# Inverted 16x16 blocks leave for DRAM and come back without the zeros between them, and are spread on chip

## The chip, the core and the metric

The kernel runs on one core of a Trainium2 chip. The metric is the device time of one execution in microseconds (us). The kernel before took 2705.86 us as the median of 3 runs (2704.35 to 2707.13).

## The reference, cut to what matters

One inference step of a trunk of two layers, for a prompt of 1024 tokens and a group of 8 samples of 4 tokens each. Layer 0 mixes with gated DeltaNet heads (and a spatial gate beside them), layer 1 with mLSTM heads; each is followed by a squared-ReLU MLP. The change lies in the DeltaNet heads alone: 4 heads, keys and values of 128.

```python
def gated_delta_rule(q, k, v, g, beta, S0):
    ...                                     # blocks of C tokens, gc = running sum of g
    kb = k * beta[..., None]
    A = jnp.where(strict, jnp.einsum('nbhid,nbhjd->nbhij', kb, k) * decay, 0.0)
    rhs = jnp.concatenate([v * beta[..., None], kb * jnp.exp(gc)[..., None]], -1)
    sol = lax.linalg.triangular_solve(jnp.eye(C) + A, rhs, left_side=True, lower=True, unit_diagonal=True)
    u_val, w_k = sol[..., :DV], sol[..., DV:]
    ...
    def step(S, xs):
        v_new = u_c - jnp.einsum('bhik,bhkv->bhiv', wk_c, S)
        o = jnp.einsum('bhik,bhkv->bhiv', qd_c, S) + jnp.einsum('bhij,bhjv->bhiv', qk_c, v_new)
        S = S * gl_c[..., None, None] + jnp.einsum('bhik,bhiv->bhkv', kd_c, v_new)
        return S, o
```

What matters is the solve with the lower triangle I + A, once for each block of tokens and each head. The kernel takes blocks of 128 tokens and computes the inverse itself.

## The kernel before, in words

**Two kinds of work.** The large matrix products (`dense` in PSUM) run with f32 inputs split into a high and a low half: ScalarE makes `whi` from a weight block that SyncE has loaded into `wst` (L1112), VectorE makes `wlo = wst - whi` (L1623), and TensorE multiplies high by high, low by high and high by low (L587). A weight block of 128x1024 is a *unit*. A unit on the first group of 512 tokens or on the second of 544 (512 + 32 sample tokens) is cut into four *pieces* (`("d", u, p)`), each of two of the eight inner steps: 6 matmuls of 512 columns, or 12 of 272. The heads' work (`mixer` in PSUM, `arena` in SBUF) is written as a second list of items.

**The order.** `Plan.mix` lays the second list evenly among the pieces of the first; an item `("rest",)` is a place with nothing in it. Every engine walks the same list in order and does its own part of each item, with semaphores between them, so the list sets the order on every queue. An engine that waits holds up all that stands behind on its own queue.

**DeltaNet by tiles.** `Plan.gdn` writes the items of each prompt tile of 128 tokens (tiles 0 to 7; tiles 0 to 3 lie beside the input projection, tiles 4 to 7 beside the first MLP). For tile t:

- `sum`, `dec`, `kk`, `kT`, `vT`: norms, decays, and A (TensorE L587, VectorE L1887).
- `kk` on GpSimd (`base_blocks`): A is written to `arow` in DRAM (L2446), and its 32 diagonal 16x16 blocks (4 heads, 8 each) are read back with one block on each of 32 partitions (L2448) into `C`.
- `b1`, `b2`, `b3` on VectorE: the 32 blocks are inverted by substitution and merging (L1845, L1847), and a transposed copy `CT` is made (L1922), which counts up the semaphore `g_inv`.
- `b3` on GpSimd: after `g_inv` it writes `C` and `CT` to the diagonals of eight 128x128 matrices `xrow` in DRAM (L2453, twice), whose other places were set to zero at the start (L2320). When both have landed it reads all eight matrices back (L2456) into `XX`: 4 plain ones (`Xi`) and 4 transposed (`XiT`).
- `la`, `lb` for the levels 4, 5 and 6: the inverse grows from blocks of 16 to 32, 64 and 128. TensorE's `la` of level 4 waits for `g_bin`, the landing of the read. VectorE masks (L1936) and adds (L1943).
- `vn`, `zw`, `o`, `oT`: the inverse meets the right-hand sides, the state `St` is carried on.

Between `b3` and the first `la` stand 3 rests. The memory of `C`, `CT` and of the scratch belongs to `SQ` and `RB` of the tile, which the next tile's `act` item (ScalarE, `w("bout", ...)`) writes again.

Of the kernel before, what the change touches and what calls it, by code (L numbers as in the profile page):

```python
# [7 lines left out]
ALU = mybir.AluOpType  # L8
# [67 lines left out]
class Plan:  # L76
# [64 lines left out]
    @staticmethod  # L141
    def gdn(tiles):
        out = []
        for i, t in enumerate(tiles):
            if i == 0:
                out += [("gx", t), ("g", t, "act", 0)] + [("g", t, "gv", 0)] * (t >= 4) + [("g", t, "sum", 0)]
            out += [("g", t, s, 0) for s in ("dec", "kk", "kT")] + [("rest",)]
            out.append(("g", t, "vT", 0))
            more = i + 1 < len(tiles)
            if more:  # L150
                out.append(("gx", t + 1))
            out += [("rest",)] * 1 + [("g", t, s, 0) for s in ("b1", "b2", "b3")] + [("rest",)] * 3
            for q in range(LB, LEVELS):
                out += [("g", t, "la", q), ("g", t, "lb", q)]
                if q == 4 and more:
                    out.append(("g", t + 1, "act", 0))
                if q == 5 and more and t + 1 >= 4:
                    out.append(("g", t + 1, "gv", 0))
            if i == 0:
                out += [("gx2", t), ("rest",), ("rest",)]  # L160
            out += [("g", t, s, 0) for s in ("vn", "zw", "o")]
            out.append(("g", t + 1, "sum", 0) if more else ("rest",))
            out.append(("g", t, "oT", 0))
            if more:
                out.append(("gx2", t + 1))
        return out
# [148 lines left out]
def build(nc, x_prompt, x_sample, state_gdn, state_gdn_conv, state_mlstm_c, state_mlstm_n, state_mlstm_m,  # L315
# [4 lines left out]
    with ctx:  # L320
# [7 lines left out]
        def sb(name, shape, dt=F32):  # L328
            return ctx.enter_context(nc.sbuf_tensor(name, shape, dt))
# [42 lines left out]
        cum = sb("cum", [P, TILES + 1, 12])  # L372
        epsc = sb("epsc", [P, 1])
        fold = sb("fold", [4 * H, 2 * H])
        ssx = sb("ssx", [P, TILES + 1])


# [39 lines left out]

        def inv_at(t, q, p):

            return t * (1 + 2 * NL) + (2 * (q - LB) + p + 2 if t < TILES else 2 * q + p + 1)  # L420

        def t2_at(t, q, p):

# [6 lines left out]
        def gdn_map(t):  # L430
            n = P if t < TILES else NS
            keys = ["X", "QH", "SQ", "RB", "DT", "QD", "XX", "KB", "KD", "RU", "VB"]
            shapes = [(NCH, n), (8, n), (8, n), (8, n), (H, n), (H, n), (2, 4, n), (H, n)] + [(H, P)] * 3
            if n == NS:
                keys += ["RW", "NW", "NWM", "QDM", "KM", "SS"]
                shapes += [(H, P), (H, n), (H, NB, NS), (H, NB, NS), (2, 4, P), (2, NB, P)]
            m = dict(zip(keys, carve(arena, *shapes)))
            m["Dm"], m["E"] = m["SQ"][:, 0:4], m["SQ"][:, 4:8]
            m["T2"], m["A"] = m["RB"][:, 0:4], m["RB"][:, 4:8]
            m["ON"], m["VN"] = m["VB"] if n == P else m["RW"], m["RU"]  # L440
            m["Xi"] = lambda h: m["XX"][0:n, 0, h, :]
            m["XiT"] = lambda h: m["XX"][0:n, 1, h, :]
            if n == P:
                sq, t2 = (m[k].rearrange("p h n -> p (h n)") for k in ("SQ", "RB"))
                m["C"], m["CT"], m["U"] = carve(sq[0:NBLK], (CB,), (WB * WB,), (WB * WB // 4,))
                m["tmp"] = t2[0:NBLK, 0:512]
            return m

# [53 lines left out]
        mrow = nc.dram_tensor("mrow", (2, 2, H, GN[1]), F32)  # L502
        grow = nc.dram_tensor("grow", (H, T), F32)
        arow = nc.dram_tensor("arow", (H, P * (P + 1)), F32)
        xrow = nc.dram_tensor("xrow", (2 * H, P * (P + 1)), F32)

        def by_token(rows):

# [76 lines left out]
        def _(pe):  # L585
# [171 lines left out]
            def gdn(t, step, q):  # L757
# [58 lines left out]
                elif step == "la":  # L816

                    r, c0 = half(q, n)
                    for p in range(2):
                        if q == LB:  # L820
                            w("bin", 32 * (t + 1))
                            if p:
                                w("ru")
                        else:
                            w("inv", inv_at(t, q - 1, p))
                        for h in (2 * p, 2 * p + 1):
                            last = mm(M4(3 * p)[0:r, h % 2, 0:r], m["A"][0:n, h, 0:r], m["XiT"](h)[:, c0:n])
                        s(last, "t2")
                        if q == LEVELS - 1:
                            for h in (2 * p, 2 * p + 1):  # L830
                                last = pe.transpose(M4(1 + p)[0:r, h % 2, 0:n], m["XiT"](h)[:, 0:r], ident[0:n, 0:n])
                            s(last, "xt")
# [270 lines left out]
        def _(act):  # L1103
# [251 lines left out]
            def gdn(t, step, q):  # L1355
# [5 lines left out]
                if step == "act":  # L1361
                    w("xin", 32 * (t + 1))
                    if t:
                        w("qd", t)
                        w("bout", 48 * t + 16)
                    if g:
                        after(own(A_(X[:, 0:12, :], X[:, 0:12, :], ACT.Silu)))
                    s(A_(m["SQ"], X[:, 0:8, :], ACT.Square), "sq")
# [233 lines left out]
        def _(dve):  # L1602
# [256 lines left out]
            def gdn(t, step, q):  # L1859
# [58 lines left out]
                elif step == "b3":  # L1918
                    if LB == 4:
                        merge_right(m, 0, 8)  # L1920
                    c = m["C"][:, 0:WB * WB].rearrange("p (i j) -> p i j", j=WB)
                    s(dve.tensor_copy(m["CT"].rearrange("p (j i) -> p i j", i=WB), c), "inv")  # L1922
                elif step == "l0":
                    for p in range(2):
                        w("t2", t2_at(t, 0, p))
# [333 lines left out]
        def _(pool):  # L2259
# [48 lines left out]
            def constants():  # L2308
# [7 lines left out]
                pool.memset(rowmask[:, :], 1.0)  # L2316
                pool.memset(colmask[:, :, :], 0.0)
                pool.memset(lmask0T[:, :], 0.0)
                step(pool.memset(lmask[:, :, :], 0.0))
                dma(by_token(xrow[:, :]), lmask[:, 0:1, :].broadcast_to([P, 2 * H, P]))\  # L2320
                    .then_inc(S("g_bout"), 16)
                for m, n in ((triU, P), (triUS, NS)):
                    step(affine(m[:, :], [[1, n]], ALU.is_ge, 0.0, 0, -1))
                for m, n in ((maskpos, P), (maskposS, NS)):
# [10 lines left out]
                    step(pool.memset(colmask[:, b, b * LS:(b + 1) * LS], 1.0))  # L2335
                v = lmask0T[:, :].rearrange("p (b e) -> p b e", e=2)
                step(affine(v[:, :, 0], [[-2, P // 2]], ALU.not_equal, 1.0, -1, 1))
                pool.wait_ge(S("g_bout"), 16)
                for q in range(LEVELS):
                    w = 1 << q  # L2340
                    v = lmask[:, q, :].rearrange("p (b e w) -> p b e w", e=2, w=w)
# [100 lines left out]
            def base_blocks(t, name):  # L2442
                m = gdn_map(t)
                if name == "kk":
                    pool.wait_ge(S("g_A"), t + 1)
                    dma(by_token(arow[:, :]), m["A"]).then_inc(S("g_bout"), 16)  # L2446
                    pool.wait_ge(S("g_bout"), 48 * t + 32)
                    dma(m["C"][:, 0:WB * WB].rearrange("p (i j) -> p i j", i=WB), diagonal(arow[:, :]))\  # L2448
                        .then_inc(S("g_bin"), 16)
                else:  # L2450
                    pool.wait_ge(S("g_inv"), t * (1 + 2 * NL) + 1)
                    for a, k in enumerate(("C", "CT")):
                        dma(diagonal(xrow[a * H:(a + 1) * H, :]), m[k][:, 0:WB * WB].rearrange("p (i j) -> p i j", i=WB))\  # L2453
                            .then_inc(S("g_bout"), 16)
                    pool.wait_ge(S("g_bout"), 48 * t + 64)
                    dma(m["XX"].rearrange("p a h n -> p (a h) n"), by_token(xrow[:, :])).then_inc(S("g_bin"), 16)  # L2456

            def gdn(t, name, q):
                if t < TILES and name in ("kk", "b3"):
                    base_blocks(t, name)  # L2460
                elif name == "vT":
                    n = tok(t)[2]
                    VB = gdn_map(t)["VB"]
# [194 lines left out]
```

## Time and profile before

| | |
|---|---|
| median of 3 runs | 2705.86 us (2704.35 to 2707.13) |
| the profiled execution | 2705.05 us, span 2703.3 us |
| mean granted TensorE clock | 0.983 |
| TensorE busy | 2597.3 us (96%) |
| VectorE busy | 1380.7 us (51%) |
| ScalarE busy | 1125.0 us (42%) |
| GpSimd busy | 256.4 us (9%) |
| HBM | 120 GB/s over the span |

Engines are named PE (TensorE; PEld is its weight load), DVE (VectorE), ACT (ScalarE), POOL (GpSimd) and SP (SyncE). L with a number is the line of the kernel. All matrix products have the line L587 of a helper, so they are told apart by what they write and read: `dense` or `mixer`. The granted clock is 1.00 at 2.4 GHz and 0.50 at 1.2 GHz; a stretch in between has parts of both. All scratch of the heads is one tile, `arena`, so its rows need the line or the shape to be told apart.

### The profile page before, as it was taken

To read this page: it belongs to the slowest core of one execution; us is meant where nothing else is said; L and a number is where in the kernel's file an instruction comes from. 1 tells how busy PE (TensorE), PEld (TensorE's weight loads), DVE (VectorE), ACT (ScalarE), POOL (GpSimd) and SP (SyncE) were. 2 spreads that over 40 slices of the span, in tenths; PEclk is the share of its full clock that TensorE was granted. 3 is DMA by queue.
4 is the path that set the end of the run, shared out by engine and by line. 5 is a ranking of instruction groups with operands and counts; after the bars stand their busy time and mean duration, and the time that the engine had idled before them with its cause. 6 is when DMAs were issued, how large, how long until landed. Compare 5 with 4: busy or idle time off the path is not lost.

```text
span 2703.3 us, 39205 instructions
## 1 busy us (share of the span) xinstructions
PE 2597.3 (96%) x16262; PEld 2311.4 (86%) x16262; DVE 1380.7 (51%) x2193; ACT 1125.0 (42%) x1913; POOL 256.4 (9%) x408
## 2 busy tenths in 40 slices
PE   7988979999999999999999999999999999999998
PEld 5767878777778788899999998998877797999998
DVE  4745664645655366534444456535554447344344
ACT  5553446544545245433333345434332344332334
POOL 5021111101101001110000001110000000000000
PEclk9998989999999999999999999999999999999999
DMA  6554324524433335543333335554434334233232
GB/s 197 158 150 120 109 85 120 171 83 114 115 95 90 94 117 176 177 147 102 98 102 102 100 87 169 170 155 125 121 121 125 114 109 134 87 109 110 88 92 80
DMA packets 370017, 325.65 MB, mean 120 GB/s; under 512 B 12074, under 2 KB 339812, under 8 KB 369841
## 3 DMA queue, kind: packets, MB, share of 16 engines
q1 hardware_dynamic: 336224, 207.91, 26.7%
q0 software_dynamic: 33616, 115.25, 14.1%
q8 instruction: 129, 2.11, 0.3%
q14 instruction: 48, 0.39, 0.0%
HBM read 265.00 MB, written 58.10 MB: 120 GB/s over the span
## 4 chain that ended last, share of the span: by engine, by line
PE 77%; DVE 6%; ACT 3%; DMA 2%; issue 1%; POOL 0%; DVEq 0%; ACTq 0%; POOLq 0%
PE dense L587 68%; PE mixer L587 7%; DVE wlo L1623 1%; DMA arena<-xrow 1%; ACT arena L1112 1%; DVE arena L1845 1%; ACT whi L1112 1%; DMA xrow<-arena 1%; DVE arena L1847 0%; DVE hf L1761 0%; ACT relu L1112 0%; DVE accA L1698 0%; DVE hlo L1757 0%; PE mixer L1033 0%; PE mixer L961 0%
## 5 line engine op out<-in xcount | busy, mean ns | idle before, releaser
L587 PE MATMUL dense<-hhi,whi 128*128 128x272 f32 (+1 forms) x3072 | 852.7, 332 | 20.1 <-DVE hlo L1757 10.1
L587 PE MATMUL dense<-hlo,whi 128*128 128x272 f32 (+1 forms) x3072 | 827.0, 323 | 0.0
L587 PE MATMUL dense<-hhi,wlo 128*128 128x272 f32 (+1 forms) x3072 | 826.8, 323 | 0.0
L1623 DVE TENSOR_TENSOR wlo<-wst,whi 128x1024 fp32r<-128x1024 f32 x384 | 472.0, 1229 | 239.5 <-ACT whi L1112 238.5
L587 PEld LDWEIGHTS dense<-hhi,whi 128*128 128x128 f32 x3072 | 517.5, 190 | 80.0 <-issue 15.3
L1112 ACT ACTIVATE whi<-wst 128x1024 fp32r<-128x1024 f32 x384 | 403.7, 1051 | 417.5 <-PE dense L587 413.9
L587 PEld LDWEIGHTS dense<-hhi,wlo 128*128 128x128 f32 x3072 | 516.0, 190 | 42.6
L587 PEld LDWEIGHTS dense<-hlo,whi 128*128 128x128 f32 x3072 | 518.5, 190 | 37.4 <-issue 0.7
L587 PE MATMUL dense<-h1hi,whi 128*128 128x272 f32 (+1 forms) x1536 | 425.1, 331 | 12.3 <-DVE wlo L1623 7.5
L587 PE MATMUL dense<-h1hi,wlo 128*128 128x272 f32 (+1 forms) x1536 | 415.2, 324 | 0.0
L587 PE MATMUL dense<-h1lo,whi 128*128 128x272 f32 (+1 forms) x1536 | 414.9, 324 | 0.0
L587 PEld LDWEIGHTS dense<-h1hi,whi 128*128 128x128 f32 x1536 | 256.6, 188 | 44.1 <-DVE wlo L1623 11.5
L587 PE MATMUL mixer<-arena 128*128 128x128 f32 (+11 forms) x1552 | 237.4, 299 | 54.2 <-DMA arena<-xrow 53.2
L1639 DVE TENSOR_TENSOR h1lo<-relu,h1hi 128x544 fp32r<-128x544 f32 (+1 forms) x128 | 90.6, 708 | 377.2 <-ACT relu L1112 377.1
L587 PEld LDWEIGHTS mixer<-arena 128*128 128x128 f32 (+5 forms) x1552 | 199.5, 178 | 94.6 <-DMA arena<-xrow 55.9
L587 PEld LDWEIGHTS dense<-h1lo,whi 128*128 128x128 f32 x1536 | 258.5, 189 | 21.3 <-issue 0.5
L587 PEld LDWEIGHTS dense<-h1hi,wlo 128*128 128x128 f32 x1536 | 256.6, 188 | 22.5
L1112 ACT ACTIVATE relu<-dense 128x512 f32<-128x512 f32 (+2 forms) x132 | 80.6, 611 | 408.3 <-PE dense L587 408.2
L1698 DVE TENSOR_TENSOR accA<-dense,accA 128x512 f32<-128x512 f32 (+1 forms) x168 | 116.5, 699 | 102.0 <-PE dense L587 101.6
L1112 ACT ACTIVATE ffh<-dense 128x512 f32<-128x512 f32 (+6 forms) x124 | 62.3, 526 | 193.5 <-PE dense L587 180.1
L1714 DVE TENSOR_TENSOR ssum<-ssum,sq 128x512 f32<-128x512 f32 (+1 forms) x98 | 69.3, 707 | 125.5 <-ACT sq L1112 125.4
L1112 ACT ACTIVATE arena<-mixer 128x128 f32<-128x128 f32 (+9 forms) x175 | 63.4, 377 | 99.6 <-PE mixer L587 58.1
(346 smaller groups left out, 1807.2 us busy)
## 6 DMA issues: line engine op xcount, KB each, us to landing
wst<-in_w_ff_dram SPq DMA_DIRECT2D x256, 512.0 KB, 4.0
wst<-in_w_in_even_dram SPq DMA_DIRECT2D x48, 512.0 KB, 4.1
wst<-in_w_in_odd_dram SPq DMA_DIRECT2D x48, 512.0 KB, 4.0
proj<-ffh POOLq DMA_DIRECT2D x48, 272.0 KB, 2.5
proj<-ffh POOLq DMA_DIRECT2D x48, 256.0 KB, 2.6
arena<-proj POOLq DMA_DIRECT2D x16, 512.0 KB, 4.9
wst<-in_w_out_even_dram SPq DMA_DIRECT2D x16, 512.0 KB, 3.7
arena<-proj POOLq DMA_DIRECT2D x8, 1024.0 KB, 7.9
```

The lines of the kernel that those rows point to most:

```text
L587: return pe.matmul(out, lhsT, rhs, start=start, stop=stop)
L1112: return act.activation(out, in_, func, **how)
L1623: TT(wlo[:, u % 2, :], wst[:, u % 2, :], whi[:, u % 2, :].bitcast(F32), ALU.subtract)\
L1639: TT(h1lo[:, k, 0:n], r, h1hi[:, k, 0:n].bitcast(F32), ALU.subtract)\
L1698: TT(v, out_of(key, g), v, ALU.add).then_inc(S("dve_evac"), 1)
L1714: ins = TT(ssum[:, 0:n], ssum[:, 0:n], sq2[:, c % 2, 0:n], ALU.add)
L1845: link(TT(tmp, left.unsqueeze(2).broadcast_to([NBLK, b, b, b]), right.rearrange("p j c -> p c j").unsqueeze(1).broadcast_to([NBLK, b, b, b ...
```

## The change

What goes to DRAM is one transfer for `C` and `CT` together, 32 partitions with two runs of 256 numbers, into an `xrow` that holds nothing but the blocks. What comes back is `D16`, 128 partitions with 8 runs of 16 numbers: for each of the 4 heads, plain and transposed, row i of block b on partition 16b + i. A new item `b4` multiplies it into `XX`: each run of 16 is repeated at the 8 block places of its row, times a mask `blkmask` (128x8) that is 1 where the row belongs to the block. VectorE does this for the transposed half, GpSimd for the plain half, and both count up `g_inv`; TensorE's first `la` waits for that count instead of the landing, and so does the next tile's `act` on ScalarE. The zeroing transfer at the start goes; a memset and two selects for the mask come. In the list of items, 5 rests and `b4` stand where 3 rests stood.

```diff
@@ Plan.gdn
-            out += [("rest",)] * 1 + [("g", t, s, 0) for s in ("b1", "b2", "b3")] + [("rest",)] * 3
+            out += [("rest",)] * 1 + [("g", t, s, 0) for s in ("b1", "b2", "b3")] + [("rest",)] * 5
+            out.append(("g", t, "b4", 0))
@@ places in SBUF and DRAM
+                m["both"] = sq[0:NBLK, 0:2 * CB].rearrange("p (a x) -> p a x", a=2)[:, :, 0:WB * WB]
+                m["D16"] = carve(sq, (2, H, WB), at=640)[0]
-        xrow = nc.dram_tensor("xrow", (2 * H, P * (P + 1)), F32)
+        xrow = nc.dram_tensor("xrow", (2, NBLK, WB * WB), F32)
@@ TensorE, la of level LB = 4
-                            w("bin", 32 * (t + 1))
+                            w("inv", t * (3 + 2 * NL) + 3)
@@ ScalarE, act of the next tile
-                        w("bout", 48 * t + 16)
+                        w("inv", inv_at(t - 1, LB, 0) - 1)
@@ VectorE
+                elif step == "b4":
+                    w("bin", 32 * t + 32)
+                    shape = [P, H, P // WB, WB]
+                    s(TT(m["XX"][:, 1].rearrange("p h (b j) -> p h b j", j=WB),
+                         m["D16"][:, 1].unsqueeze(2).broadcast_to(shape),
+                         blkmask[:, :].unsqueeze(1).unsqueeze(3).broadcast_to(shape), ALU.mult), "inv")
@@ GpSimd, base_blocks after b3
-                    for a, k in enumerate(("C", "CT")):
-                        dma(diagonal(xrow[a * H:(a + 1) * H, :]), m[k][:, 0:WB * WB].rearrange("p (i j) -> p i j", i=WB))\
-                            .then_inc(S("g_bout"), 16)
-                    pool.wait_ge(S("g_bout"), 48 * t + 64)
-                    dma(m["XX"].rearrange("p a h n -> p (a h) n"), by_token(xrow[:, :])).then_inc(S("g_bin"), 16)
+                    dma(xrow[:, :, :].rearrange("a p x -> p a x"), m["both"]).then_inc(S("g_bout"), 16)
+                    pool.wait_ge(S("g_bout"), 32 * t + 32)
+                    dma(m["D16"].rearrange("p a h j -> p (a h) j"),
+                        xrow[:, :, :].rearrange("a (h b) (i j) -> (b i) (a h) j", h=H, j=WB)).then_inc(S("g_bin"), 16)
@@ GpSimd, b4 (and the constants: blkmask made, the zeroing transfer taken out)
+                elif name == "b4":
...
+                    pool.wait_ge(S("g_bin"), 32 * t + 32)
+                    pool.tensor_tensor(m["XX"][:, 0].rearrange("p h (b j) -> p h b j", j=WB),
+                                       m["D16"][:, 0].unsqueeze(2).broadcast_to(shape),
...
+                        .then_inc(S("g_inv"), 1)
```

**What it does to the order.** In pieces of dense work in the list: between `b1` and the first `la` stood 6, 5, 5, 5, 10, 10, 10, 10 pieces for tiles 0 to 7, now 9, 7, 6, 7, 14, 14, 14, 14. From `vT` to the first `la` TensorE's queue had 54, 84, 72, 90, 90, 90, 78 dense matmuls for tiles 0, 1, 3, 4, 5, 6, 7 (tile 2 has the gate's products among them), now 66, 108, 96, 114, 108, 108, 102. The number of pieces is the same over the whole, so other gaps have fewer.

VectorE's queue in tile 5, from the transposed copy (L1922, now L1926) to the transpose after level 4. Before (`h1lo` is the low half of the MLP's hidden activations, one for each unit of its first product):

```order
L1922 COPY arena<-arena 32x16x16
L1639 TENSOR_TENSOR h1lo<-relu,h1hi 128x512
L1623 TENSOR_TENSOR wlo<-wst,whi 128x1024
L1639 TENSOR_TENSOR h1lo<-relu,h1hi 128x512
L1623 TENSOR_TENSOR wlo<-wst,whi 128x1024
L1936 TENSOR_TENSOR arena<-mixer,lmask 128x256 x2
L1943 TENSOR_TENSOR arena<-arena,mixer 128x256 x2
L1947 STREAM_TRANSPOSE arena<-arena 128x256 x2
```

And now:

```order
L1926 COPY arena<-arena 32x16x16
L1643 TENSOR_TENSOR h1lo<-relu,h1hi 128x512
L1627 TENSOR_TENSOR wlo<-wst,whi 128x1024
L1643 TENSOR_TENSOR h1lo<-relu,h1hi 128x512
L1627 TENSOR_TENSOR wlo<-wst,whi 128x1024
L1643 TENSOR_TENSOR h1lo<-relu,h1hi 128x512
L1930 TENSOR_TENSOR arena<-arena,blkmask 128x512
L1627 TENSOR_TENSOR wlo<-wst,whi 128x1024
L1946 TENSOR_TENSOR arena<-mixer,lmask 128x256 x2
```

One more unit's work stands between the copy and the first mask, and the spread of the transposed half (L1930) stands within it.

VectorE's queue in tile 1, from right behind the transposed copy on, where the dense work is the input projection with its convolution (`ffh<-ffh,par`). Before:

```order
L1653 COPY ffh<-ffh 128x3
L1656 COPY ffh<-ffh 128x8x3
L1623 TENSOR_TENSOR wlo<-wst,whi 128x1024
L1662 SCALAR_TENSOR_TENSOR ffh<-ffh,par 128x512
L1665 SCALAR_TENSOR_TENSOR ffh<-ffh,par 128x32
L1662 SCALAR_TENSOR_TENSOR ffh<-ffh,par 128x512
L1665 SCALAR_TENSOR_TENSOR ffh<-ffh,par 128x32
L1936 TENSOR_TENSOR arena<-mixer,lmask 128x256 x2
```

And now:

```order
L1666 SCALAR_TENSOR_TENSOR ffh<-ffh,par 128x512
L1669 SCALAR_TENSOR_TENSOR ffh<-ffh,par 128x32
L1677 COPY ffh<-ffh 128x3
L1678 COPY ffh<-ffh 128x24
L1657 COPY ffh<-ffh 128x3
L1660 COPY ffh<-ffh 128x8x3
L1627 TENSOR_TENSOR wlo<-wst,whi 128x1024
L1666 SCALAR_TENSOR_TENSOR ffh<-ffh,par 128x512
L1669 SCALAR_TENSOR_TENSOR ffh<-ffh,par 128x32
L1666 SCALAR_TENSOR_TENSOR ffh<-ffh,par 128x512
L1669 SCALAR_TENSOR_TENSOR ffh<-ffh,par 128x32
L1930 TENSOR_TENSOR arena<-arena,blkmask 128x512
```

One more step of the convolution stands ahead of the spread, and one step and the end of a unit behind it, ahead of the first mask.

GpSimd's queue in tile 5, from the loads of the next tile on. Before:

```order
L2402 DMA arena<-grow 128x4x128
L2453 DMA xrow<-arena 32x16x16 x2
L2456 DMA arena<-xrow 128x8x128
L2408 DMA arena<-proj 128x8x128
L2446 DMA arow<-arena 128x4x128
```

And now:

```order
L2412 DMA arena<-grow 128x4x128
L2462 DMA xrow<-arena 32x2x256
L2464 DMA arena<-xrow 128x8x16
L2474 TENSOR_TENSOR arena<-arena,blkmask 128x512
L2418 DMA arena<-proj 128x8x128
L2456 DMA arow<-arena 128x4x128
```

The two writes have become one, and the spread of the plain half stands right behind the read, with the late loads of the next tile behind it.

## Rows read from the trace of the kernel before

**Rows 1.** Waits of PE, longest first: total us, times, longest.

```profile
PE mixer L587 <- DMA arena<-xrow: 53.2, 8, 12.0
PE dense L587 <- DVE wlo L1623: 16.7, 15, 3.5
```

**Rows 2.** PE in order of time: start us, us, [idle before], tiles 0 to 7.

```profile
185.90 1.44 PE L587 MATMUL mixer<-arena 128*128 128x128 f32 x5 [9.97 <-DMA arena<-xrow]
...
253.40 1.86 PE L587 MATMUL mixer<-arena 128*128 128x128 f32 x7 [12.01 <-DMA arena<-xrow]
...
316.83 1.43 PE L587 MATMUL mixer<-arena 128*128 128x128 f32 x5 [3.51 <-DMA arena<-xrow]
...
378.58 1.65 PE L587 MATMUL mixer<-arena 128*128 128x128 f32 x6 [10.35 <-DMA arena<-xrow]
...
550.95 1.43 PE L587 MATMUL mixer<-arena 128*128 128x128 f32 x5 [5.39 <-DMA arena<-xrow]
...
644.02 1.37 PE L587 MATMUL mixer<-arena 128*128 128x128 f32 x5 [3.56 <-DMA arena<-xrow]
...
728.37 0.82 PE L587 MATMUL mixer<-arena 128*128 128x128 f32 x5 [1.66 <-DMA arena<-xrow]
...
811.75 1.65 PE L587 MATMUL mixer<-arena 128*128 128x128 f32 x6 [6.71 <-DMA arena<-xrow]
```

**Rows 3.** Stretches behind these waits: from:to, us, PE busy, granted clock, DMA share, GB/s.

```profile
185.90:192.00 6.10, 6.10 (x26) 0.65 0.00 0
253.40:260.00 6.60, 6.60 (x36) 0.62 0.11 43
316.83:322.00 5.17, 5.17 (x31) 0.71 0.04 8
378.58:386.00 7.42, 7.42 (x38) 0.59 0.26 72
550.95:557.00 6.05, 6.05 (x23) 0.63 0.10 27
644.02:649.00 4.98, 4.98 (x19) 0.66 0.25 87
811.75:817.00 5.25, 5.25 (x21) 0.71 0.01 3
```

**Rows 4.** PE in order of time, dense matmuls at full clock.

```profile
192.77 0.39 PE L587 MATMUL dense<-hlo,whi 128*128 128x512 f32 x1
193.00 0.40 PE L587 MATMUL dense<-hhi,wlo 128*128 128x512 f32 x1
```

**Rows 5.** POOL in order of time, tile 1.

```profile
245.38 1.32 POOL L2453 DMA_DIRECT2D xrow<-arena  x2 [1.68 <-DVE arena L1922]
248.80 0.89 POOL L2456 DMA_DIRECT2D arena<-xrow  x1 [2.11 <-DMA xrow<-arena]
```

**Rows 6.** DMA issues: queue, count, KB each, median us from issue to landing.

```profile
arena<-xrow POOLq DMA_DIRECT2D x8, 512.0 KB, 5.1
...
xrow<-arena POOLq DMA_DIRECT2D x16, 32.0 KB, 2.1
...
arena<-arow POOLq DMA_DIRECT2D x8, 32.0 KB, 2.2
```

**Rows 7.** Groups by shape from 140 to 830 us: count, busy us, mean ns, idle before.

```profile
L1662 DVE SCALAR_TENSOR_TENSOR ffh<-ffh,par 128x512 f32<-128x512 f32 x36 | 27.9, 775 | 0.4
...
L1897 DVE TENSOR_TENSOR arena<-arena 128x512 f32<-128x512 f32 x8 | 5.5, 682 | 0.0
...
L2467 POOL TENSOR_TENSOR arena<-arena 128x512 f32<-128x512 f32 x8 | 10.4, 1302 | 0.1
```

**Rows 8.** POOL and DVE in order of time, tile 1, an overlap.

```profile
234.22 1.30 POOL L2467 TENSOR_TENSOR arena<-arena 128x512 f32<-128x512 f32 x1
234.23 1.84 DVE L1662 SCALAR_TENSOR_TENSOR ffh<-ffh,par 128x512 f32<-128x512 f32 x1
```

**Rows 9.** Stretch before tile 3's wait, all engines: PE, PEld, DVE, ACT, POOL busy (x), clock, DMA.

```profile
340.00:372.00 32.00, 25.93 (x199) 24.35 (x197) 27.05 (x65) 18.41 (x50) 5.58 (x7) 0.99 0.34 95
```

## What the change will do, written before it ran

> **What bounds the kernel now.** I read the table of busy times first: TensorE works 2597.3 us of a span of 2703.3, so all its idle time together is 106 us, and no change off its path can pay more than that. The next view is TensorE's waits. Half of the idle time has one cause: the first `la` of each of the eight prompt tiles waits for the landing of `xrow`, 53.2 us in 8 waits; the next cause, the low halves of the weights, has 16.7 us [rows 1]. In order of time the eight waits are 9.97, 12.01, 3.51, 10.35 us (tiles 0 to 3) and 5.39, 3.56, 1.66, 6.71 us (tiles 4 to 7) [rows 2]. The reader is to see that the first four sum to 35.8 and the last four to 17.3.
>
> The stretches behind the waits show a second cost. TensorE is busy without a gap there, but at a granted clock between its two levels: 0.65, 0.62, 0.71, 0.59, 0.63, 0.66 and 0.71 [rows 3], where it is 1.00 soon after. After idle time TensorE runs on at 1.2 GHz for some us. Length times (1 - clock) is what that costs: 2.1, 2.5, 1.5, 3.0, 2.2, 1.7, 1.5, together 14.5 us. Tile 6, with the shortest wait, has none.
>
> So at most 53.2 + 14.5 = 68 us hang on these landings.
>
> **The sum, part by part.** I count against the profiled execution, 2705.05 us (span 2703.3 and 1.7 around it), which is 0.8 under the median.
>
> *1. More dense work ahead of `la`.* Consecutive matmuls of 512 columns start 0.23 us apart at full clock [rows 4], so a piece of 6 takes 1.38 us, and one of 12 by 272 columns about 1.46 (an estimate by columns).
>
> Tiles 4 to 7: from `b1` to `la` there are 14 pieces where there were 10, which is 5.5 us. VectorE reaches `b1` by the order of its queue there (A's blocks have long landed), so all that follows, the inverse and both transfers, runs against these pieces. 5.5 covers 5.39, 3.56 and 1.66; of 6.71 some 1 us may stay, less what the inverse gains from having one piece's work less between its own steps. I take 17.0 of 17.3. With the waits goes the low clock behind them: 2.2 + 1.7 + 1.5 = 5.4.
>
> Tiles 0 to 3: there the inverse hangs on `kk`, since `arow` goes out and comes back right before it and VectorE starts as soon as it can. From `vT` to `la` the dense matmuls rise by 12 (tile 0: 2 pieces of 1.38 = 2.8), by 24 of 272 columns (tile 1: 2.9) and by 24 (tile 3). In tile 3 one piece went away between `kk` and `kT`, so from `kk` it is one piece, 1.5; tile 2 also one, 1.5. Sum 8.7 of 35.8. The waits of tiles 0, 1 and 3 stay over 6 us each, and I leave the low clock behind them as it is.
>
> *2. The round trip.* In tile 1 GpSimd starts the writes at 245.38, the read at 248.80, and TensorE goes on at 253.40 [rows 5, 2]: 3.4 + 4.6 = 8.0 us. One issue instead of two saves half of the 1.32 that the pair takes, 0.66. The write has 64 KB in runs of 1 KB; a write of 32 KB in runs of 64 bytes lands in 2.1 [rows 6], and I expect no more. The read had 1024 runs of 512 bytes and landed in 5.1; now it has 1024 of 64 bytes. No row shows that shape. The nearest below is the read of `arow`, 512 runs of 64 bytes, 2.2; above, 5.1 if the count of runs sets the time. I take 3.3, nearer to the row with the same run. That saves 1.8 (0 to 2.9).
>
> DMA: Bandwidth & Descriptors (Specifications) in the Trainium skill speaks against this part: below 512 bytes a transfer is less than line rate, with read-modify-write. The run of 64 bytes is what it warns of; the rows show only that 512 such runs land in 2.2, less than half of what 1024 runs of 512 bytes take, and by the rule the upper end, 5.1, would be the likelier one: 1.8 more in each of four tiles, a sum of 21.1 and 2684.8, inside the forecast's own range.
>
> *3. The spread.* A VectorE product of two SBUF operands of 128x512 takes 0.68, GpSimd's takes 1.30 [rows 7]. In tiles 0 to 3 both engines are through with their earlier work when the read lands, and start together. What happens then can be seen in tile 1: GpSimd's product ran from 234.22 to 235.52, and a VectorE operation of 128x512 begun at 234.23 took 1.84 instead of its mean 0.775 [rows 8, 7]: it got hardly anything done until GpSimd had finished. So the pair costs 1.30 + 0.68 = 2.0 on the path, not 1.3. The repeated operands have no row; I bound it from 1.3 (no overlap) to 2.6 (each half as long again).
>
> This is what SBUF — State Buffer (Who interferes with whom) in the Trainium skill says: a VectorE instruction with two SBUF inputs contends with a GpSimd instruction that reads SBUF, and one blocks. By that rule, the trace agrees (1.84 against 0.775), and dividing the spread between the two engines saves nothing while they start together; without it the pair would take 1.30 and the sum would be 2.7 larger, 2675.
>
> The round trip with the spread: -0.66 - 1.8 + 2.0 + 0.1 for one more semaphore = -0.3 us per tile (bounds -2.2 and +2.1). It counts in tiles 0 to 3: 1.2 (from 8.8 down to -8.4). In tiles 4 to 7 GpSimd spreads at once and VectorE about a piece before `la`.
>
> *4. What it takes.* (a) `la` now depends on VectorE's place in its queue. In tiles 5 and 6 `b4` is one piece ahead of `la` (1.38 us), and VectorE first has an addition or a low half of 0.7 behind the piece before, then 0.68: about even. I take 0.5 per tile in tiles 4 to 7, 2 us in all (0 to 4). (b) The pieces come out of other gaps: between levels 4 and 5 tiles 4 and 7 have one piece between `la` and `lb` where they had two, between levels 5 and 6 some have none. The levels already run at one piece in tiles 0 to 3, with next to no wait there, so I take 0.25 per tile, 2 us (up to rival 2). (c) VectorE's 8 products are 5.5 us of an engine that is 51% busy, hidden but for (a). (d) The start: a transfer issue less, a memset and two small selects more on GpSimd, even.
>
> Sum: 17.0 + 5.4 + 8.7 + 1.2 - 2 - 2 = 28.3 us. From 2705.05 that is 2676.8, and 2677.6 on the footing of the median. Forecast 2678; its own range is 2670 to 2686 by the bounds of the trip and of 4.
>
> **Rivals.**
>
> *Rival 1, the round trip becomes much shorter.* The read lands in 2.2 and the spreads hardly disturb each other: -2.2 in each of tiles 0 to 3, 8.8 instead of 1.2; no wait for VectorE in tiles 4 to 7 (2 more), and tile 2's wait of 3.51 goes with its low clock (1.5 more). 28.3 + 7.6 + 2 + 1.5 = 39.4: 2666. For it: 64 KB instead of 512, beside weight loads. Against: the count of runs is the same.
>
> *Rival 2, tiles 0 to 3 are paced by VectorE.* Before tile 3's wait VectorE is busy 27.05 of 32 us, TensorE 25.93 [rows 9]. If the gap that lost the pieces then waits for VectorE, the 8.7 of those tiles and the 1.2 come back as waits elsewhere, and the same loss of a piece costs another 3 in tiles 4 to 7: 28.3 - 12.9 = 15.4, 2690.
>
> *Rival 3, slower.* The rests add no work, they move it: 2 + 2 + 1 + 1 pieces of about 1.45 and 16 of 1.38, 31 us of cover, leave the gaps between the levels, the output and the next tile's `kk`. If those gaps are as tight as this one, each us comes back as a wait there, and VectorE's 8 products (5.5) stand in the same chains. Then 17.0 + 5.4 + 8.7 + 1.2 = 32.3 gained, 31 + 5.5 lost: +4, and with one or two new stretches of low clock at about 2 us each 2712. It decides when over 27 of the 31 return. Against it: the waits list has only small waits of mixer work beside `xrow`, and levels one piece apart run now.
>
> *Rival 4, no change.* A middle of 2 and 3: around 27 us lost to the gaps, within 0.2% of before (5.4 us, about what a measurement of this kernel can tell from no change).
>
> **Chances.** Forecast 0.60; rival 1 0.13; rival 2 0.15; rival 3 0.07; rival 4 0.05. Faster by over 0.2% holds for the first three, 0.88; same 0.05; slower 0.07. The range for 8 in 10 takes in the forecast and most of rivals 1 and 2: 2664 to 2694.
>
> **What would show it.** In the profile after: TensorE's waits for the spread (VectorE's L1930 or GpSimd's L2474 as releaser) under 1 us in tiles 4 to 7 and 6 to 9 us in tiles 0, 1 and 3, in sum 25 to 29; clock 1.00 behind tiles 4 to 7; the new read landing between 2.2 and 5.1; VectorE's product about 1.9 in tiles 0 to 3 and 0.7 in tiles 4 to 7. New waits of over 1 us at `lb`, `zw`, `dec` or `kk` in many tiles would speak for rival 2 or 3. The forecast is wrong if tiles 4 to 7 still wait, or if the small waits in sum grow by over 10 us.

## The result, and the profile after

The changed kernel took 2661.6 us, median of 4 runs (2660.3 to 2662.1), beside 2705.1 (2704.2 to 2707.1, 4 runs) for the kernel before on the same chip: a ratio of 0.9837, 95% interval 0.9820 to 0.9854. The forecast was 2678 in a range of 2664 to 2694; the time lies below the range, 16 us under the forecast. The gain is 43.5 us where 28 were worked out. The profiled execution's span fell from 2703.3 to 2658.5, and TensorE is busy 97% of it.

The waits of TensorE after, in the columns of [rows 1]:

```profile
PE dense L591 <- DVE wlo L1627: 25.5, 19, 5.3
...
PE mixer L591 <- DVE arena L1930: 9.6, 3, 8.1
...
PE mixer L591 <- POOL arena L2474: 1.8, 1, 1.8
```

L1930 and L2474 are the two halves of the spread; lines of before have moved down by 4. The 53.2 us in 8 waits have become 11.4 in 4. Waits for `wlo`, the low halves of the weights, have grown from 16.7 to 25.5: a part of the idle time has only changed its name. All of TensorE's idle time outside the waits for the landing or the spread grew by 11 us (106.0 - 53.2 = 52.8 before, 75.4 - 11.4 = 64.0 after). In order of time, all waits for the spread and the one large wait for `wlo` (tiles 0, 1, 3, 3, 5):

```profile
184.48 1.16 PE L591 MATMUL mixer<-arena 128*128 128x128 f32 x8 [1.83 <-POOL arena L2474]
...
248.20 2.07 PE L591 MATMUL mixer<-arena 128*128 128x128 f32 x8 [8.09 <-DVE arena L1930]
...
356.80 0.82 PE L591 MATMUL dense<-hhi,whi 128*128 128x272 f32 x2 [5.26 <-DVE wlo L1627]
...
362.90 1.16 PE L591 MATMUL mixer<-arena 128*128 128x128 f32 x8 [0.81 <-DVE arena L1930]
...
618.85 1.16 PE L591 MATMUL mixer<-arena 128*128 128x128 f32 x8 [0.69 <-DVE arena L1930]
```

Beside [rows 2]: 9.97, 12.01, 3.51 and 10.35 us became 1.83, 8.09, none and 0.81 in tiles 0 to 3, and 17.3 in sum became 0.69 in tiles 4 to 7. Tile 3 has kept over half of its wait in another form, the 5.26 for `wlo`.

GpSimd in order of time (start us, us, what it waited for), the round trip of tiles 0 to 3; first the write, then the read, and for tiles 0 and 1 GpSimd's half of the spread:

```profile
177.47 0.55 POOL L2462 DMA_DIRECT2D xrow<-arena  x1 [3.25 <-DVE arena L1926]
179.68 0.92 POOL L2464 DMA_DIRECT2D arena<-xrow  x1 [1.66 <-DMA xrow<-arena]
182.87 1.55 POOL L2474 TENSOR_TENSOR arena<-arena,blkmask 128x512 f32<-128x512 f32 x1 [1.70 <-DMA arena<-xrow]
...
239.95 0.55 POOL L2462 DMA_DIRECT2D xrow<-arena  x1 [9.53 <-DVE arena L1926]
242.59 0.92 POOL L2464 DMA_DIRECT2D arena<-xrow  x1 [2.09 <-DMA xrow<-arena]
246.55 1.05 POOL L2474 TENSOR_TENSOR arena<-arena,blkmask 128x512 f32<-128x512 f32 x1 [2.47 <-DMA arena<-xrow]
...
297.95 0.55 POOL L2462 DMA_DIRECT2D xrow<-arena  x1 [4.69 <-DVE arena L1926]
300.14 0.92 POOL L2464 DMA_DIRECT2D arena<-xrow  x1 [1.65 <-DMA xrow<-arena]
...
356.00 0.55 POOL L2462 DMA_DIRECT2D xrow<-arena  x1 [3.67 <-DVE arena L1926]
358.20 0.93 POOL L2464 DMA_DIRECT2D arena<-xrow  x1 [1.65 <-DMA xrow<-arena]
```

The same rows of the kernel before, tiles 0, 2 and 3 (tile 1 is in [rows 5]):

```profile
175.33 1.41 POOL L2453 DMA_DIRECT2D xrow<-arena  x2 [5.21 <-DVE arena L1922]
180.84 0.89 POOL L2456 DMA_DIRECT2D arena<-xrow  x1 [4.10 <-DMA xrow<-arena]
...
307.13 1.33 POOL L2453 DMA_DIRECT2D xrow<-arena  x2 [4.95 <-DVE arena L1922]
311.68 0.89 POOL L2456 DMA_DIRECT2D arena<-xrow  x1 [3.22 <-DMA xrow<-arena]
...
370.37 1.32 POOL L2453 DMA_DIRECT2D xrow<-arena  x2 [9.37 <-DVE arena L1922]
373.41 0.90 POOL L2456 DMA_DIRECT2D arena<-xrow  x1 [1.72 <-DMA xrow<-arena]
```

The reader should subtract the starts. From the write to the read it is 2.2, 2.6, 2.2, 2.2 us after the change. Before, it is 5.5, 3.4, 4.6, 3.0 over the same four tiles. That is the step which the prediction expected to change by 0.66 only.

VectorE's half in tiles 0 and 1, start and us:

```profile
182.82 0.69 DVE L1930 TENSOR_TENSOR arena<-arena,blkmask 128x512 f32<-128x512 f32 x1 [1.69 <-DMA arena<-xrow]
...
246.57 1.57 DVE L1930 TENSOR_TENSOR arena<-arena,blkmask 128x512 f32<-128x512 f32 x1 [2.83 <-DMA arena<-xrow]
```

The engine that starts second is the one that is stretched: in tile 0 VectorE is first and takes 0.69 while GpSimd takes 1.55; in tile 1 GpSimd is first by 0.02 and takes 1.05 while VectorE takes 1.57. Either way the pair is over in about 1.6 us, not 2.0.

The DMA issues, in the columns of [rows 6]:

```profile
xrow<-arena POOLq DMA_DIRECT2D x8, 64.0 KB, 1.9
arena<-xrow POOLq DMA_DIRECT2D x8, 64.0 KB, 3.2
arena<-arow POOLq DMA_DIRECT2D x8, 32.0 KB, 3.3
```

Stretches that hold the four trips (from:to, length, PE busy, granted clock, DMA share, GB/s):

```profile
175.00:200.00 25.00, 21.64 (x129) 1.00 0.49 140
240.00:270.00 30.00, 21.84 (x170) 0.89 0.29 86
310.00:330.00 20.00, 19.52 (x156) 1.00 0.29 90
330.00:365.00 35.00, 28.93 (x215) 0.90 0.32 89
365.00:424.00 59.00, 57.63 (x359) 1.00 0.41 114
```

Only tiles 1 and 3 still have low clock behind a wait. Right behind the two waits that are left it is

```profile
248.20:254.00 5.80, 5.80 (x33) 0.66 0.26 99
356.80:363.00 6.20, 5.39 (x25) 0.63 0.55 151
```

or (1 - clock) times length, 2.0 + 2.3 = 4.3 us, where [rows 3] had 2.1 + 2.5 + 1.5 + 3.0 = 9.1 in tiles 0 to 3, and 5.4 in tiles 4 to 7, which is gone.

**Where the 44.8 us of span came from.** The dense matmuls are the same in both kernels and, but for a dozen of the 14059, in the same order, so the starts of the one with the same number can be compared. From the dense matmul that starts at 110.7 in both, to the one at 424.4 before and 404.7 after, tiles 0 to 3 gained 19.7 us. From there to 976.2 and 934.8, tiles 4 to 7 and the sample's tile, it is another 21.8. The rest of the program gained 3.4, spread over some 1700 us. TensorE's own busy time tells what kind of gain it is. In tiles 0 to 3 it fell from 270.4 to 267.1 us, so 3.3 of the 19.7 is busy time of the same work, as less of it ran at the low clock, and some 16.5 is idle time: the waits for the landing or the spread fell by 25.1, and those for `wlo` grew by 8.8. In tiles 4 to 7 it fell from 525.56 to 517.42, 8.1 of the 21.8; the waits for the landing or the spread fell by 16.6, and others grew by 3.0. The same kernel profiled again (`e0_again` below) gives 18.3, 21.7 and 5.5 for the three parts, so a difference of one or two us between two profiles tells nothing.

### The profile page after: what moved, and what is told of

Its sections match the earlier page's. It is cut to its first block, busy times and chain, and to the rows that moved or that the text cites. A ratio compares the mean times of both kernels' runs of the same rounds, so it can differ in the third digit from the quotient of the medians.

```text
span 2658.5 us, 39212 instructions
## 1 busy us (share of the span) xinstructions
PE 2583.1 (97%) x16262; PEld 2302.1 (87%) x16262; DVE 1384.5 (52%) x2201; ACT 1127.4 (42%) x1915; POOL 259.3 (10%) x410
## 4 chain that ended last, share of the span: by engine, by line
PE 84%; DVE 7%; ACT 5%; issue 2%; DMA 2%; POOL 0%; DVEq 0%; ACTq 0%
PE dense L591 74%; PE mixer L591 8%; DVE wlo L1627 2%; ACT arena L1116 1%; ACT whi L1116 1%; DVE hf L1765 1%; DVE arena L1849 1%; DVE hlo L1761 1%; DMA proj<-ffh 0%; DVE ffh L1666 0%; ACT relu L1116 0%; ACT ffh L1116 0%; DVE arena L1851 0%; ACT L1116 0%; PE mixer L655 0%
## 5 line engine op out<-in xcount | busy, mean ns | idle before, releaser
L591 PE MATMUL mixer<-arena 128*128 128x128 f32 (+11 forms) x1552 | 230.8, 293 | 13.9 <-DVE arena L1930 9.6
L591 PEld LDWEIGHTS mixer<-arena 128*128 128x128 f32 (+5 forms) x1552 | 193.5, 173 | 53.2 <-issue 20.8
L1702 DVE TENSOR_TENSOR accA<-dense,accA 128x512 f32<-128x512 f32 (+1 forms) x168 | 116.3, 698 | 106.0 <-PE dense L591 105.5
```

The lines of the kernel that those rows point to most:

```text
L591: return pe.matmul(out, lhsT, rhs, start=start, stop=stop)
L1702: TT(v, out_of(key, g), v, ALU.add).then_inc(S("dve_evac"), 1)
```

## The experiments

All ratios are to the kernel before, run on the same chip in turn; in brackets the 95% interval. "Tiles 0 to 3" and "tiles 4 to 7" are gains by dense matmuls of the same number, as above; the sample's tile is counted with the latter. In the expectations theory A gives most of the gain to the order of the work, and a part that can be measured to the transfers; theory B gives most to the transfers. `e1_order`, `e2_trip`, `e4_eight` and `e3_vector` ran on one chip, with 2707.2 us for before; `e0_again`, `e5_runs`, `e7_split` and `e8_early` on one with 2706.5; `e3_pool` with 2707.7.

**The order alone (`e1_order`).** The kernel before, with six rests where it had three; transfers and zeros as before. The first `la` then stands at the same place of the list as in the changed kernel.

```
-... [("g", t, s, 0) for s in ("b1", "b2", "b3")] + [("rest",)] * 3
+... [("g", t, s, 0) for s in ("b1", "b2", "b3")] + [("rest",)] * 6
```

Expected: 

> The kernel before with 6 rests where it had 3, transfers as before: the order of the change alone. Theory A (order and trip each carry a part): tiles 4 to 7 lose their waits of 17.3 us but for about 2 and the low clock behind them, 5.4; tiles 0 to 3 gain the moved dense work, 10 us, and keep most of their low clock: 29 to 33 us, 2672 to 2676. Theory B (the shorter trip is what pays, and moved pieces come back as waits in other gaps): 10 to 15 us, 2690 to 2695.

Measured: 2680.1 us (2677.9 to 2682.8), ratio 0.9904 [0.9889, 0.9918]: between the two theories. Tiles 4 to 7 gained 20.3, nearly all that the full change gains there, and no wait for `xrow` is left in them. Tiles 0 to 3 gained 3.3. TensorE in order of time in those:

```profile
189.81 2.08 PE L587 MATMUL mixer<-arena 128*128 128x128 f32 x8 [6.14 <-DMA arena<-xrow]
...
257.31 2.07 PE L587 MATMUL mixer<-arena 128*128 128x128 f32 x8 [9.30 <-DMA arena<-xrow]
...
368.40 0.82 PE L587 MATMUL dense<-hhi,whi 128*128 128x272 f32 x2 [6.47 <-DVE wlo L1623]
...
378.24 2.07 PE L587 MATMUL mixer<-arena 128*128 128x128 f32 x8 [4.75 <-DMA arena<-xrow]
```

With 0.20 us in tile 2, the waits for `xrow` fell by 15.4 us, from 35.8 to 20.4. But in tile 3 the wait of 10.35 became 6.47 for `wlo` and 4.75 for `xrow`, 11.2 in all: the pieces that were moved ahead came to the engine before VectorE had made their low halves, so nothing was gained there. Most of the low clock stayed too. (1 - clock) times length over the stretches of the list above is 3.5 + 5.1 + 7.1 = 15.7 us, idle time included, from granted clocks of 0.86 (175 to 200 us), 0.83 (240 to 270) and 0.88 (365 to 424) and 1.00 in the other two, against 3.3 + 3.5 = 6.8 with the whole change. By itself the order did in tiles 0 to 3 what rival 2 said.

**The transfers alone (`e2_trip`).** The changed kernel with two rests ahead of `b4` instead of five. `b4` is an item of the list too, so two rests and `b4` take the place of the three rests of before, and `la` stands where it stood.

```
-... + [("rest",)] * 5
+... + [("rest",)] * 2
 out.append(("g", t, "b4", 0))
```

Expected: 

> The changed kernel with 2 rests and the spread where before had 3 rests, so that la stands where it stood: the new round trip alone. Theory A: the trip from the first write to go is 1.5 to 2 us shorter than before in the mean of the eight tiles, which gives 13 to 16 us and 2 to 4 us of low clock: 2685 to 2691. Theory of the prediction: the trip with its spread is only 0.3 us shorter, 2702 to 2704. Theory B: over 25 us, under 2680.

Measured: 2683.2 us (2681.7 to 2685.0), ratio 0.9915 [0.9900, 0.9929]. The prediction had 1.2 us for this part and is refuted: tiles 0 to 3 gained 9.6, tiles 4 to 7 gained 8.9. The time lies a little below theory A's range, with 5.5 us behind the tiles. The waits for the spread are 7.89, 11.24, 0.60 and 8.42 us in tiles 0 to 3 and 11.5 in sum in tiles 4 to 7. From the write to the read it is 2.2 to 3.7 us.

So in tiles 4 to 7 the order gives 20.3, the transfers 8.9, and both together 21.8: the order alone is cover enough for nearly all of it, the transfers alone give some two fifths. In tiles 0 to 3 it is the other way about: 3.3 and 9.6 apart, and 19.7 together (18.3 in `e0_again`), 5.4 to 6.8 more than their sum. Up to 4 of these 7 are low clock: (1 - clock) times length over the five stretches is 20.8 us before, 15.7 with the order, 15.7 with the transfers, and 6.8 with both, so both take off 14.0 and not 10.2 (some of it in idle time, so this is an upper end). TensorE's busy time in these tiles, which leaves the idle part out, is 270.4 us before, 272.4 with the order, 268.4 with the transfers and 267.1 with both: apart they add 2.0 and take off 2.0, together they take off 3.3.

**The writes as they were (`e5_runs`), beside the changed kernel again (`e0_again`).** The changed kernel, with its compact read, but the inverted blocks written as before in two writes of 512 runs of 64 bytes, into rows of 128 bytes, from which the read takes its 64.

```
-xrow = nc.dram_tensor("xrow", (2, NBLK, WB * WB), F32)
+xrow = nc.dram_tensor("xrow", (2, NBLK, WB, 2 * WB), F32)
-dma(xrow[:, :, :].rearrange("a p x -> p a x"), m["both"]).then_inc(S("g_bout"), 16)
+for a, k in enumerate(("C", "CT")):
+    dma(xrow[a, :, :, 0:WB], m[k][:, 0:WB * WB].rearrange("p (i j) -> p i j", i=WB))...
```

Expected: 

> The changed kernel, but the blocks go out as before, in two writes of 512 runs of 64 bytes (into rows padded to 128 bytes); the read of D16 and the spread stay. Theory A (the pair of scattered writes was the slow part of the old trip, 3.0 to 6.2 us from the first write to the read, against 2.2 to 2.7 now): the trip grows by 1.5 us in the mean, and tiles 0, 1 and 3, which still wait, lose 4 to 7 us with some low clock: 2666 to 2671. Theory of the prediction (only the second issue of 0.66 us counts): 2 to 3 us, 2663 to 2665.

Expected of the second run of the changed kernel: 

> The changed kernel once more, as the yardstick on this chip for the three kernels beside it: 2660 to 2664.

Measured: `e0_again` 2660.0 us (2658.5 to 2662.3), ratio 0.9828 [0.9813, 0.9843]; `e5_runs` 2670.2 (2668.5 to 2670.6), ratio 0.9864 [0.9849, 0.9878], 10.1 us slower, as theory A had it. GpSimd's writes and reads of tiles 0, 1 and 3:

```profile
177.95 1.30 POOL L2463 DMA_DIRECT2D xrow<-arena  x2 [3.26 <-DVE arena L1926]
182.62 0.92 POOL L2466 DMA_DIRECT2D arena<-xrow  x1 [3.37 <-DMA xrow<-arena]
...
246.57 1.31 POOL L2463 DMA_DIRECT2D xrow<-arena  x2 [9.68 <-DVE arena L1926]
249.59 0.91 POOL L2466 DMA_DIRECT2D arena<-xrow  x1 [1.71 <-DMA xrow<-arena]
...
364.07 1.30 POOL L2463 DMA_DIRECT2D xrow<-arena  x2 [3.66 <-DVE arena L1926]
368.58 0.92 POOL L2466 DMA_DIRECT2D arena<-xrow  x1 [3.21 <-DMA xrow<-arena]
```

From the first write to the read it is 4.7, 3.0 and 4.5 us, over the eight tiles 4.1 in the mean, as before the change (4.0), and 2.4 with it. All of the loss that is in the tiles is in tiles 0 to 3, 8.2 us against `e0_again`; tiles 4 to 7 lost nothing. The two writes of tile 0, one after the other, with the time to landing at the end:

```profile
xrow<-arena POOLq DMA_DIRECT2D x1, 32.0 KB, 2.1
xrow<-arena POOLq DMA_DIRECT2D x1, 32.0 KB, 3.4
```

The first write lands in 2.1 us in seven of the eight tiles, hardly later than the one compact write of the changed kernel (1.9). The second lands in 2.1 in three tiles (1, 2 and 5), in 2.7 in tile 7, and in 3.4 to 4.1 in the other four. The loss follows this. Tile 1's write starts 6.6 us later than in `e0_again` (246.57 against 240.00), tile 3's again 6.6 (364.07 against 357.43), and tile 3's first `la` 8.6: tile 0 lost 6, tiles 1 and 2 nothing, tile 3 two. So the two writes are worth 1.7 us per tile in the trip, nothing where the second lands at once or where dense work covers it. Whether the second is late because it is a second transfer, or because 1024 short runs are under way, isn't shown: one write of 1024 runs of 64 bytes did not run.

**Both halves on VectorE (`e3_vector`), both on GpSimd (`e3_pool`).**

```
 elif step == "b4":                          # VectorE, in e3_vector
+    s(TT(m["XX"][:, 0]..., m["D16"][:, 0]..., blkmask..., ALU.mult), "inv")
...
 pool.wait_ge(S("g_bin"), 32 * t + 32)       # GpSimd, in e3_pool
+pool.tensor_tensor(m["XX"][:, 1]..., m["D16"][:, 1]..., blkmask..., ALU.mult)
```

In both, the product of the other engine is taken out.

Expected: 

> The changed kernel with both halves spread by VectorE, one after the other, none by GpSimd. If the two engines block one another, 2 x 0.69 = 1.4 us take the place of the 1.57 that the overlapped product took in tiles 1 and 3, and nothing is lost: within 2 us of the change. If they ran beside one another and the 1.57 were something else, the path would grow by 0.7 us in tiles 0 to 3, and VectorE's queue by 0.7 in tiles 4 to 7: 2 to 5 us slower.

Expected: 

> The changed kernel with both halves of the spread given to GpSimd in all eight tiles. Theory (the two engines block each other only in part: the divided spread takes 1.57 us in tiles 1 and 3, where a single half takes 1.05 on GpSimd and 0.69 on VectorE): GpSimd needs 2.1 us for both halves, so the read's landing to the first la grows by 0.5 us in tiles 0 to 3, while la no longer depends on VectorE's queue; 0 to 2.5 us slower than the changed kernel, 2660 to 2664. Rival (the queue of VectorE is what holds la in tiles 0 and 1): without it the waits before la shrink by over 1 us each and the kernel is 2 us or more faster, under 2658.

Measured: `e3_vector` 2661.8 us (2660.7 to 2662.7), ratio 0.9834 [0.9818, 0.9850], level with the change. VectorE's two products overlap a little, and the pair takes 1.3 us (184.17 to 185.46 in tile 0), less than the 1.6 of the divided pair. Dividing the spread between two engines saves nothing against VectorE alone. `e3_pool` 2667.3 us (2664.6 to 2667.9), ratio 0.9846 [0.9833, 0.9859]: slower by more than I expected, and not faster as the rival had it. The profile tells a part of why. GpSimd's halves and VectorE in tile 3:

```profile
364.81 1.06 POOL L2472 TENSOR_TENSOR arena<-arena,blkmask 128x512 f32<-128x512 f32 x1 [0.91 <-DMA arena<-xrow]
365.82 2.04 POOL L2476 TENSOR_TENSOR arena<-arena,blkmask 128x512 f32<-128x512 f32 x1
```

```profile
364.81 2.13 DVE L1627 TENSOR_TENSOR wlo<-wst,whi 128x1024 fp32r<-128x1024 f32 x1 [1.47 <-issue]
366.87 1.54 DVE L1666 SCALAR_TENSOR_TENSOR ffh<-ffh,par 128x512 f32<-128x512 f32 x1
```

VectorE doesn't stand idle while GpSimd spreads: it goes on to the next `wlo` and the convolution, and each blocks the other. The low half takes 2.13 instead of 1.19 to 1.23, GpSimd's second product 2.04 instead of 1.05, and the spread is over 3.05 us after its start instead of 1.6. I had left that out. In tiles 0, 1 and 2 the spread takes 2.1, 2.5 and 2.1. TensorE's waits for the spread and the `wlo` wait of tile 3 are together 2.9 us longer in tiles 0 to 3 than in the changed kernel; what else makes up the loss isn't shown.

**More rests (`e4_eight`, `e7_split`).** Eight rests ahead of `b4` instead of five, in all tiles, or in tiles 0 to 3 alone.

```
-... + [("rest",)] * 5
+... + [("rest",)] * 8                        # e4_eight
+... + [("rest",)] * (8 if t < 4 else 5)      # e7_split
```

Expected: 

> The changed kernel with 8 rests ahead of the spread instead of 5. Theory A: what is left of the waits in tiles 0, 1 and 3 (1.8, 8.1 and 5.3 us with 2.0 + 2.1 us of low clock) shrinks by one or two pieces of 1.45 us in each, nothing is left to win in tiles 4 to 7: 4 to 8 us faster than the change, 2653 to 2658. Rival (the other gaps have no slack left): waits of mixer work and of the weights' low halves grow by as much, 2660 or more.

Expected: 

> The changed kernel with 8 rests in tiles 0 to 3 and 5 in tiles 4 to 7. With 8 in all tiles the first four gained 2.8 us more and the last four and the sample tile gave about 0.7 back, where no wait was left to cover. Theory: 3 to 5 us faster than the change, level with 8 rests everywhere or 1 us better. Rival: the gain of 8 rests came from tiles 4 to 7 after all: within 1 us of the change.

Measured: `e4_eight` 2657.9 us (2657.1 to 2658.9), ratio 0.9821 [0.9806, 0.9836]; `e7_split` 2657.8 (2656.9 to 2659.3), ratio 0.9820 [0.9805, 0.9834]. `e7_split` is 2.2 us under `e0_again` on the same chip, a little less than expected; the intervals of the ratios overlap, so the gain is likely but not certain. What limits it is seen in `e4_eight`, TensorE in order of time, tiles 0 to 3:

```profile
173.68 0.50 PE L591 MATMUL dense<-hhi,whi 128*128 128x512 f32 x1 [2.45 <-DVE wlo L1627]
...
240.02 0.52 PE L591 MATMUL dense<-hhi,whi 128*128 128x272 f32 x2 [2.42 <-DVE wlo L1627]
247.50 1.16 PE L591 MATMUL mixer<-arena 128*128 128x128 f32 x8 [1.21 <-DVE arena L1930]
...
355.03 0.82 PE L591 MATMUL dense<-hhi,whi 128*128 128x272 f32 x2 [5.08 <-DVE wlo L1627]
```

The wait of 8.09 for the spread in tile 1 is down to 1.21, and 2.42 for `wlo` stands ahead of it. The 5.08 in tile 3 is there as it was (5.26), and a wait of 2.31 us for VectorE's L1982, at 218 us, is new.

**The low halves earlier (`e8_early`).** `e7_split`, and VectorE makes the low half of the unit's next weights ahead of the inverse's steps, in the two units where such a step stands between the unit's first two pieces: tile 0's `b1`, tile 1's `b2` and `b3`. Tiles 2 and 3 are left as they were.

```
-if item[2] == 1:
+if item[2] == (item[1] not in EARLY):
     lo(item[1] + 1)
```

Expected: 

> As the kernel with 8 and 5 rests, and VectorE makes the low half of the next unit's weights ahead of the inverse's steps where these stood between (one unit each in tiles 0 and 1, where TensorE waited 2.4 us for it in each). Theory: TensorE's idle time in a tile is set by the chain from A through the inverse, the trip and the spread, so a wait for the weights that goes comes back as a wait for the spread: within 1.5 us of the kernel without it. Rival: the waits for the weights stand by themselves: 3 to 5 us faster.

Measured: 2657.9 us (2656.8 to 2658.1), ratio 0.9818 [0.9802, 0.9835], the same as `e7_split`. The wait for `wlo` is gone in tile 1 (2.48 us in `e7_split`) and down from 2.94 to 1.53 in tile 0, and the waits for the spread are back (lines are down by 3 here):

```profile
185.16 1.16 PE L594 MATMUL mixer<-arena 128*128 128x128 f32 x8 [2.24 <-POOL arena L2477]
...
247.39 2.07 PE L594 MATMUL mixer<-arena 128*128 128x128 f32 x8 [4.28 <-DVE arena L1933]
```

Whichever VectorE does first, the low half or the inverse, the other is late. What is left in tiles 0 and 1 is thus the length of VectorE's queue together with the trip, not its order. Tile 3's wait for `wlo`, 5.06 us here, was not touched by this edit, and whether another order would shorten it is open. These three kernels, at about 2657.8 us, are the best that ran.

## Why the prediction was wrong

The mechanism was right: dense work ahead of `la` covers the landing, and the waits go away with the low clock behind them. The sizes in tiles 0 to 3 were not. The time is that of rival 1, 2666, and beyond it, but not by its cause: rival 1 had the read landing in 2.2 us, and it took 3.2. Point by point:

- **Tiles 4 to 7.** Predicted 17.0 + 5.4, less 3 for new waits (2 for VectorE, 1 of the pieces missing elsewhere): 19.4. Measured 21.8. The waits for the spread are 0.69 in all and no low clock is left behind them. The new waits came as priced, 3.0 us (1.9 of them for ScalarE, though, which I had not named). What was too small is the term for the low clock: TensorE's busy time fell by 8.1 us, not 5.4. `e1_order` shows that the order alone is enough here, as the prediction had it.
- **The round trip, the step that failed.** "One issue instead of two saves half of the 1.32 that the pair takes, 0.66" is a sum of issue times. What the second write really cost was landing. I had taken the 2.1 us of [rows 6], the time of one write of 32 KB, for both, and tile 1, whose 3.4 us is one of the shortest of the eight, for the typical tile. In tile 1 itself the saving was 0.8, close to the 0.66. Over all eight, write to read was 4.0 us before and 2.4 after: 1.6 instead of 0.66. `e5_runs` puts the two writes back and with them 4.1 us, and 10.1 us of time; there a second write lands up to 4.1 us after its issue.
- **The read.** Predicted 3.3, measured 3.2, against 5.1. The rule of the Trainium skill that I weighed (DMA: Bandwidth & Descriptors, Specifications) is less than line rate below 512 bytes. The trace agrees with it on the rate: 512 KB in 5.1 us is 100 KB per us, 64 KB in 3.2 us is 20. What didn't come is the time that I had hung on it, 5.1: eight times fewer bytes in as many runs landed sooner. The row below was weaker than it looked, too: 2.2 us is the median of the reads of `arow`, and single ones took 2.2 to 5.0 in the kernel before.
- **The spread.** Predicted 2.0 for the pair, measured about 1.6 (1.57 and 1.55 for the one that is second). The rule of the Trainium skill's page SBUF — State Buffer (Who interferes with whom), that one of two such instructions blocks, the trace bears out in both directions, and `e3_vector` and `e3_pool` show what follows. With the write and the read, the way from the first write to `la` was 10.6, 8.0, 9.7 and 8.2 us before [rows 2, 5] and 7.0, 8.2, 7.4 (to the end of VectorE's half; `la` doesn't wait) and 6.9 after: 6.9 us in four tiles where the sum had 1.2. Tile 1 gained nothing, since its read landed only after 3.9 us.
- **"I leave the low clock behind them as it is."** 9.1 us became 4.3, since the waits of tiles 0 and 3 fell to 1.8 and, in tile 3, 5.3 + 0.8. I had held them to be over 6 us each. This is a term at zero that depended on the sum of the other two.
- **Dense work in tiles 0 to 3.** Predicted 8.7. In `e1_order` these pieces took 15.4 us off the waits for `xrow` and gave back nearly all of it: 6.47 for `wlo` in tile 3, 0.8 to 1.7 each at four places ahead of it, and a good part of the low clock still there. That is rival 2, in one place. With the shorter trip the same pieces pay, though 8.8 us come back as waits for `wlo` there too. So the two terms can't be measured apart, and my adding of them was the second fault: 3.3 + 9.6 is not 19.7. The prediction had named small waits that grow by over 10 us in sum as a sign of its being wrong, and over the whole program they grew by 11.
- **Tile 3's wait for VectorE.** Behind the 5.26 us lies a queue: VectorE does the inverse and the convolution from 344 to 355.3 and only then the low half that TensorE waits for.

```profile
355.33 0.37 DVE L1926 COPY arena<-arena 32x256 f32<-32x256 f32 x1
355.56 1.19 DVE L1627 TENSOR_TENSOR wlo<-wst,whi 128x1024 fp32r<-128x1024 f32 x1
```

- **The rest, 3.4 us after the tiles.** Not predicted, and its cause is open. It is busy time, not waits: 1708.7 us before, 1704.8 after, at a granted clock of 1.00 in both. The same stretch gained between 1.9 and 5.7 us in the versions with the new transfers, and lost 0.6 in `e1_order`, in steps of some tenths without a single place. The changed kernel alone gave 3.4 and 5.5, so one profile of each is too little to tell a cause from variation.

Of the 16.5 us that the forecast lacked, 10.8 lie in tiles 0 to 3 (19.7 against 8.9, which is 8.7 + 1.2 less 1 for new waits), 3.4 behind the tiles, and 2.4 in tiles 4 to 7, where it is low clock.

## What to carry to other kernels

Read a wait at each of its occurrences, not at one: the middle of one tile, or one transfer's landing, hid that the trip with two writes back to back took 3.0 to 6.2 us up to the read. Where a wait can be shortened from both sides, by more cover ahead of it and by a shorter chain behind it, ask which engine feeds the cover; here the cover alone returned as a wait for VectorE's low halves, and only the two together took tile 0's wait down to 1.83 us, with a granted clock of 1.00 behind it. A term entered as "stays as it is" should be bounded by what the other terms do to it.

## What was not expected of the hardware

- Two writes of 32 KB in 512 runs of 64 bytes each, issued within 1.3 us, let the next read start 3.0 to 6.2 us after the first issue (kernel before, `e1_order`, `e5_runs`); one write of the same 64 KB in runs of 1 KB, 2.2 to 2.8, and in `e2_trip` 3.7 and 3.1 in two tiles. It is the second write that was slow and variable: over these three kernels the first landed in 2.1 us in 21 of 24 tiles, the second in 2.1 to 4.9, in 11 of 24 over 3.4. The run of 64 bytes by itself is not what was slow: a first write of 32 KB in such runs lands in 2.1, the write of 64 KB in runs of 1 KB in 1.9.
- A read of 1024 runs of 64 bytes landed in 3.2 us (median; 2.8 in `e5_runs`, from rows padded to 128 bytes), of 1024 runs of 512 bytes in 5.1: neither the bytes nor the runs alone set it.
- Two tensor products of 128x512, begun within 0.05 us on VectorE and GpSimd, end after 1.55 to 1.6 us, whoever is first: 0.69 with 1.55, 1.05 with 1.57. That is 0.1 to 0.2 under the sum of the two alone (0.69 + 1.05 = 1.74).
- GpSimd's product with a repeated operand takes 1.05, the one of two full tiles 1.30 [rows 7].
